# Rotation and copies of queries and keys one step sooner, 12 projection pieces ahead of the loop, mixing weights spread by matmuls

## The chip, the cores and the metric

The kernel runs on one core of one Trainium2 chip. The metric is device time in microseconds (us) of one execution. Beside three runs of the kernel before there is one more execution, taken with the hardware profiler; all durations below come from that one.

## What is computed

A decoder block over 2048 tokens of width 1024, all in float32: RMSNorm, one input projection, four heads of a gated linear recurrence (HGRN2), eight heads of causal dilated window attention, an output projection, the residual and a last RMSNorm. The change touches the attention part only:

```python
q = rope(at_q.reshape(B, S, AT_HEADS, AT_HEAD_DIM), positions)
k = rope(at_k.reshape(B, S, AT_HEADS, AT_HEAD_DIM), positions)
for window, dilation in ((128, 1), (512, 4), (2048, 16)):
    o_i, lse_i = dilated_window_attention(q, k, v, window, dilation)
mix_w = softmax(stack(lses), axis=0)
o_at = sum(mix_w * stack(outs)) * silu(at_z)
```

The kernel computes the windows of 512 and 2048 together as one "far" part, beside a "near" part for the window of 128, and mixes the two.

## The kernel before

**Stages.** A prologue normalises and transposes x and splits it into high and low halves (`u_hi`, `u_lo`). A second stage does the recurrence, beside its projections. A dense stage projects the values of the attention. Then comes the attention loop, and last the output projection. Every projection is three matmuls (high by high, high by low, low by high) for each of 8 slices of the contraction.

**The attention loop** goes over 64 steps `T`. Four steps `i` = 0 to 3 make a block `n` (16 blocks of 512 queries of two heads); four blocks `g` = 0 to 3 make a unit `v` (two heads). The far part of a query tile has `g`+1 key tiles, so steps grow longer with `g`.

Every engine runs its own loop over `T`, in the order in which it is written out, with semaphores between them:

- **TensorE (PE)**, in step `T`: `scores` (near at L758, far at L765) of tile `T`; transposes of the probabilities of tile `T`-1 (`turn_near_far0` at L781 and L789, `turn_far1` at L797); `weigh` of tile `T`-1 (L811, L819). Six "filler" pieces of projections stand between them, each three matmuls of 512 columns (L710 to L712): for block `n`+1 the pieces `A` and `B` (the two halves of queries and keys before rotation), for block `n` the pieces `Z` (the gate). `AHEAD` pieces run ahead of the loop, which sets where in a block each piece stands. They take turns between two PSUM banks: `B` of block `n` waits until the gate of block `n`-2 has been read (`z_done`), `Z` of block `n` until the first half of the rotation of block `n`+1 has been (`a_read`). In step `i` = 1 PE also spreads the mixing weights of the block before (`spread_weights`, L832).
- **VectorE (DVE)**: `lows` (masking, with row minima, L1488), `take_far0` (a PSUM copy), the rotation (`rope_a` in step 0, `rope_b` in step 1, both at L1251), `queries_keys_lo` (low halves, step 2), the mixing weights (`differences`, `mix_weights`, step 0), `weigh_outputs` (step 1), and the product that finishes the gate (L1566, step 3).
- **ScalarE (ACT)**: exponentials (L999), copies from PSUM (`take_near`, `take_far1`, `take_output`), `queries_keys_hi` (step 2), the tanh of the gate (L1055, step 3), high halves of the next unit's weights (`split_unit_hi`, L898), and it issues the copies of keys into `ks` (`gather_keys`, L316; step 2, in the last block of a unit step 3).
- **GpSimd (POOL)**: `combine` (step 1) and low halves of the next unit's weights (`split_unit_lo`, L1111).
- **SyncE (SP)** issues the other DMAs in one in-order queue. It waits for the end of PE's step (`pv_mm`) before it loads values (L461, L453) for the next. At the end of step 2 come the store of the output of block `n`-1 (`store_output`, L436), then the copies of the next block's queries into `qd` (L467), first half 0, then, past the scores of step 3, half 1; then the rotation table (L443). Far statistics go through DRAM at the end of step 3 and back in step 0 (L534, L507).

The tile `gate` is a single buffer: the tanh of block `n` waits until the store of block `n`-1 has landed (`comb_stored`), since `combine` leaves its result there. `r1`, `t1`, `t2`, `t3` share their room with `turned`, from which the copies read.

## Time and profile before

| what | value |
| --- | --- |
| runs of the kernel (3) | 1493.76, 1493.96, 1496.74 us; median 1493.96 us |
| profiled execution, its own time | 1488.3 us |
| its span, first to last instruction | 1486.5 us |
| busy share of the span | PE 91%, PE weight load 79%, DVE 52%, ACT 31%, POOL 21% |
| mean granted TensorE clock | 0.962 of full |
| attention loop, 659 to 1270 us | 611 us, granted clock 0.94 |

The profiled execution is 5.7 us faster than the median of the runs, and the 1.8 us between its time and its span lie outside of the instructions. "Busy" of PE counts a matmul from start to modelled end, so matmuls overlap in it. A row of the timeline gives the start, the time until the last of its instructions ends, and in brackets how long the engine was idle before, with what ended that.

### The profile page before, as it was taken

Reading aid. Unit: us, or ns where it says so; the run is one execution under the profiler, and the core shown is the slowest. Engines: PE = TensorE matmul, PEld = TensorE weight load, DVE = VectorE, ACT = ScalarE, POOL = GpSimd, SP = SyncE. Lnnn points to the kernel's source line nnn. Section 1 sums busy time; section 2 is a strip of 40 time slices with the busy share of each in tenths; the row PEclk is TensorE's granted clock in tenths of the full one; section 3 lists DMA queues with packets and bytes.
Section 4 is the critical chain, followed back from the end, with each engine's and each line's share of the span. In section 5 each row is a group of like instructions: output and inputs, shape, how many; then the busy total and the mean of one; then the engine's idle time right before and its main releaser. Section 6 shows DMA issues by size and latency. Waiting matters only on the chain.

```text
span 1486.5 us, 24236 instructions
## 1 busy us (share of the span) xinstructions
PE 1346.7 (91%) x8616; PEld 1174.3 (79%) x8616; DVE 774.7 (52%) x1933; ACT 466.4 (31%) x1328; POOL 314.8 (21%) x377
## 2 busy tenths in 40 slices
PE   5999989989999998899988888889988897599997
PEld 5989979989898998797767777677776776488886
DVE  6846847774783775215554455545555554332332
ACT  6622221122122121124444344434433444411221
POOL 5733333243243121100110002100111001110010
PEclk9999999999999999999999999999999999699999
DMA  6420230122022013413343334433323336434341
GB/s 199 144 73 22 72 103 19 43 76 78 31 76 79 22 49 102 121 38 77 106 116 92 83 101 115 99 77 89 90 70 85 83 90 196 144 112 143 128 138 61
DMA packets 115568, 135.39 MB, mean 91 GB/s; under 512 B 19584, under 2 KB 85376, under 8 KB 115456
## 3 DMA queue, kind: packets, MB, share of 16 engines
q1 hardware_dynamic: 109504, 121.81, 28.3%
q10 hardware_dynamic: 5952, 12.06, 2.8%
q8 instruction: 74, 1.21, 0.4%
q14 instruction: 38, 0.31, 0.1%
HBM read 79.18 MB, written 29.49 MB: 73 GB/s over the span
## 4 chain that ended last, share of the span: by engine, by line
PE 40%; DMA 8%; SPq 5%; DVE 3%; issue 1%; ACT 1%; ACTq 1%; POOL 0%; POOLq 0%; DVEq 0%
PE bank L577 5%; DMA qd<-turned 5%; PE bank L579 5%; PE bank L578 5%; PE bank L710 4%; PE bank L712 4%; PE bank L711 4%; SPq L467 3%; PE bank L765 3%; PE bank L819 3%; PE bank L758 2%; DVE o_nf L1251 2%; PE bank L811 2%; DMA ks<-turned 1%; PE bank L781 1%
## 5 line engine op out<-in xcount | busy, mean ns | idle before, releaser
L577 PE MATMUL bank<-w_hi,u_hi 128*128 128x256 f32 x768 | 222.4, 290 | 8.9 <-POOL w_lo L1104 4.8
L578 PE MATMUL bank<-w_lo,u_hi 128*128 128x256 f32 x768 | 219.0, 285 | 0.0
L579 PE MATMUL bank<-w_hi,u_lo 128*128 128x256 f32 x768 | 218.9, 285 | 0.0
L1488 DVE CUSTOM_DVE_ANT_0 p_near<-bank,near_m 128x256 f32<-128x256 f32 (+1 forms) x128 | 48.2, 414 | 259.9 <-PE bank L781 157.2
L577 PEld LDWEIGHTS bank<-w_hi,u_hi 128*128 128x128 f32 x768 | 149.0, 194 | 11.3 <-POOL w_lo L1104 5.3
L1251 DVE TENSOR_TENSOR room<-room 128x256 f32<-128x256 f32 (+6 forms) x386 | 136.0, 400 | 41.9 <-POOL room L1168 38.2
L578 PEld LDWEIGHTS bank<-w_lo,u_hi 128*128 128x128 f32 x768 | 149.1, 194 | 0.2
L579 PEld LDWEIGHTS bank<-w_hi,u_lo 128*128 128x128 f32 x768 | 148.9, 194 | 0.0
L710 PE MATMUL bank<-u_hi,w_hi 128*128 128x512 f32 x256 | 116.3, 454 | 4.0 <-issue 4.0
L1194 POOL TENSOR_TENSOR o_nf<-o_nf 128x512 f32<-128x512 f32 x16 | 25.5, 1591 | 420.5 <-DVE o_nf L1251 420.5
L1009 ACT COPY pT<-bank 128x512 f32<-128x512 f32 x60 | 35.2, 587 | 249.3 <-PE bank L781 226.3
L577 PE MATMUL bank<-wo_hi,mT_hi 128*128 128x512 f32 x256 | 101.9, 398 | 7.4 <-DVE mT_lo L1251 7.4
L577 PE MATMUL bank<-u_hi,w_hi 128*128 128x512 f32 x256 | 101.2, 395 | 7.9 <-issue 4.8
L712 PE MATMUL bank<-u_hi,w_lo 128*128 128x512 f32 x256 | 107.9, 421 | 0.0
L711 PE MATMUL bank<-u_lo,w_hi 128*128 128x512 f32 x256 | 107.4, 419 | 0.0
L758 PE MATMUL bank<-ks,qd 128*128 128x256 f32 (+1 forms) x256 | 53.9, 327 | 52.8 <-DMA qd<-turned 41.8
L579 PE MATMUL bank<-wo_hi,mT_lo 128*128 128x512 f32 x256 | 100.4, 392 | 0.0
L578 PE MATMUL bank<-wo_lo,mT_hi 128*128 128x512 f32 x256 | 100.3, 392 | 0.0
L579 PE MATMUL bank<-u_hi,w_lo 128*128 128x512 f32 x256 | 99.9, 390 | 0.0
L578 PE MATMUL bank<-u_lo,w_hi 128*128 128x512 f32 x256 | 99.7, 389 | 0.0
L765 PE MATMUL bank<-ks,qd 128*128 128x128 f32 (+3 forms) x256 | 92.5, 367 | 0.0
L758 PEld LDWEIGHTS bank<-ks,qd 128*128 128x128 f32 x256 | 37.7, 200 | 67.2 <-DMA ks<-turned 28.1
(164 smaller groups left out, 2958.8 us busy)
## 6 DMA issues: line engine op xcount, KB each, us to landing
qd<-turned SPq DMA_DIRECT2D x64, 256.0 KB, 5.8
stage<-in_w_groups SPq DMA_DIRECT2D x44, 256.0 KB, 3.9
room<-in_x SPq DMA_DIRECT2D x16, 512.0 KB, 4.4
values_gates<-vg_tile SPq DMA_DIRECT2D x64, 128.0 KB, 1.7
room<-values_gates SPq DMA_DIRECT2D x16, 512.0 KB, 4.5
tab<-in_rope SPq DMA_DIRECT2D x16, 512.0 KB, 6.1
xr<-in_x SPq DMA_DIRECT2D x16, 512.0 KB, 5.0
out<-hh SPq DMA_DIRECT2D x16, 512.0 KB, 3.0
```

Source lines behind the costliest of these rows:

```text
L467: sp.dma_start(qd[(2 * n + h) % Q_SLOTS][64 * z:64 * z + 64, :, :].bitcast(F32).rearrange("p a b -> p (a b)"), src[:, None, :].to_broadcas ...
L577: nc.tensor.matmul(dst, lhs_hi(k), rhs_hi(k), start=(k == 0), stop=False)
L578: nc.tensor.matmul(dst, lhs_hi(k), rhs_lo(k), start=False, stop=False)
L579: last = nc.tensor.matmul(dst, lhs_lo(k), rhs_hi(k), start=False, stop=(k == KT_N - 1))
L710: yield nc.tensor.matmul(bk[:, :], wh[:, k, :], u_hi[:, k, sl], start=(k == 0), stop=False)
L711: yield nc.tensor.matmul(bk[:, :], wh[:, k, :], u_lo[:, k, sl], start=False, stop=False)
L712: last = nc.tensor.matmul(bk[:, :], wl[:, k, :], u_hi[:, k, sl], start=False, stop=(k == KT_N - 1))
L758: last = nc.tensor.matmul(dst, q[h][:, z, j * P:(j + 1) * P], key_tiles(h, T), start=(z == 0), stop=(z == 1))
L765: last = nc.tensor.matmul(bank[2 + h][:, 0:P * (g + 1)], q[h][:, z, j::CH], keys, start=(z == 0), stop=(z == 1))
L819: last = nc.tensor.matmul(bank[6][hs, P:2 * P], far_v[:, far_slot(T, kk) % FAR_SLOTS, hs], pT[1 + h][:, kk, :], start=(kk == 0), stop=(kk ...
L1251: return nc.vector.tensor_tensor(dst, a_, b_, op)
L1488: nc.vector.tensor_tensor_reduce(out=dst, in0=src, in1=msk, scale=1.0, scalar=3e38, op0=ALU.add, op1=ALU.min, accum_out=stt[:, j, h:h + 1] ...
```

## The change

- `queries_keys_hi`, `queries_keys_lo`, the key copies of blocks other than a unit's last and the first half of the query copies move from step 2 to step 1; `rope_b` moves from step 1 to step 0, behind `mix_weights`.
- `mix_weights` leaves 128x8 weights in `ea` and `eb`, and no longer spreads them over 128x512. `spread_weights` does that by 16 matmuls, with a weight column repeated 64 times as the stationary operand and the identity as the moving one, in place of 8 transposes.
- The tanh of the gate moves from the middle of step 3 to the end of step 2 on ACT, and the product on DVE to the start of step 3. The store of the output stays at the end of step 2 on SP.
- `AHEAD` goes from 6 to 12 pieces. The rotation table's load and the next unit's weights (loads and splits) move with them.

```diff
@@ -284,7 +284,7 @@
         out_stored = [out_stored0, out_stored1]
 
         fill = filler_parts()
-        AHEAD = 6
+        AHEAD = 12
 
         def fillers(tile, first, many):
 
@@ -494,21 +494,17 @@
                 if i == 3 and n + 1 < AT_BLOCKS:
                     after(s_ready, 3 * T + 3)
                     gather_queries(n + 1, 1)
-                    if n + 2 < AT_BLOCKS:
-                        after(b_read, n + 2)
-                        load_table(n + 2)
-                if i == 3 and g == 1 and v + 1 < AT_UNITS:
-                    load_unit_piece(unit_pieces(v + 1)[0])
-                    load_unit_piece(unit_pieces(v + 1)[1])
                 if i == 0 and n >= 1:
                     after(stat_stored, 16 * n)
                     if n >= 3:
                         after(wts_ready, n - 2)
                     sp.dma_start(st_farn[(n - 1) % 2][:, :, :],
                                  stat_dram[n - 1].rearrange("(c t w) -> t c w", c=CH, w=4)).then_inc(stat_landed, 16)
-                if i == 0 and g == 3 and v + 1 < AT_UNITS:
-                    load_unit_piece(unit_pieces(v + 1)[4])
-                    load_unit_piece(unit_pieces(v + 1)[5])
+                if i == 1 and n + 1 < AT_BLOCKS:
+                    after(qk_lo, n + 2)
+                    if n >= 1:
+                        after(s_ready, 12 * n)
+                    gather_queries(n + 1, 0)
                 if T >= 1:
                     after(pv_mm, T)
                     load_far(T)
@@ -517,18 +513,16 @@
                             after(vg_stored[z], (DENSE + 2) * 128)
                     if T + 1 < AT_TILES:
                         load_near(T + 1)
-                if i == 2:
-                    if n >= 1:
-                        after(comb_done, n)
-                        store_output(n - 1)
-                    if n + 1 < AT_BLOCKS:
-                        after(qk_lo, n + 2)
-                        if n >= 1:
-                            after(s_ready, 12 * n)
-                        gather_queries(n + 1, 0)
-                    if g == 2 and v + 1 < AT_UNITS:
-                        load_unit_piece(unit_pieces(v + 1)[2])
-                        load_unit_piece(unit_pieces(v + 1)[3])
+                if i == 1 and n + 2 < AT_BLOCKS:
+                    after(b_read, n + 2)
+                    load_table(n + 2)
+                if i == 2 and n >= 1:
+                    after(comb_done, n)
+                    store_output(n - 1)
+                if v + 1 < AT_UNITS and (g, i) in ((1, 2), (2, 1), (2, 3)):
+                    z = ((1, 2), (2, 1), (2, 3)).index((g, i))
+                    load_unit_piece(unit_pieces(v + 1)[2 * z])
+                    load_unit_piece(unit_pieces(v + 1)[2 * z + 1])
                 if i == 3:
                     after(e_done, 4 * T + 4)
                     sp.dma_start(stat_dram[n].rearrange("(i w) -> i w", i=P),
@@ -823,13 +817,15 @@
             def spread_weights(n):
 
                 pe.wait_ge(wts_ready, n + 1)
-                for f, w in enumerate((r1, t3)):
+                for f, w in enumerate((ea, eb)):
                     if f == 0:
                         pe.wait_ge(pt_near_far1, 8 * (n + 1))
                     else:
                         pe.wait_ge(pt_far0, 4 * (n + 1))
                     for j in range(CH):
-                        last = nc.tensor.transpose(bank[4 + f][:, j * P:(j + 1) * P], w[:, j * P:(j + 1) * P], ident[:, :])
+                        for h in range(2):
+                            last = nc.tensor.matmul(bank[4 + f][HD * h:HD * h + HD, j * P:(j + 1) * P],
+                                                    w[:, j, h:h + 1].to_broadcast([P, HD]), ident[:, :], start=True, stop=True)
                     last.then_inc(wt_mm, 1)
 
             for T in range(AT_TILES):
@@ -1038,7 +1034,7 @@
                 v, g = divmod(n, BLOCKS)
                 if T >= 1:
                     take_near(T - 1)
-                if i == 2 and n + 1 < AT_BLOCKS:
+                if i == 1 and n + 1 < AT_BLOCKS:
                     queries_keys_hi(n + 1)
                 if T < AT_TILES:
                     exps(T, 0)
@@ -1048,22 +1044,22 @@
                     gather_keys(nc.scalar, n + 1)
                 if T >= 1:
                     take_far1(T - 1)
-                if i == 3:
-                    act.wait_ge(z_ready, n + 1)
-                    if n >= 1:
-                        act.wait_ge(comb_stored, 16 * n)
-                    nc.scalar.activation(gate[:, :], bank[filler_bank("Z", n)][:, :], ACT.Tanh, scale=0.5).then_inc(th_done, 1)
                 if i == 0 and 1 <= n < AT_BLOCKS:
                     exp_differences(n - 1)
                 if T < AT_TILES:
                     exps(T, 1)
                 if T >= 1:
                     take_output(T - 1)
-                if i == 2 and g != 3 and n + 1 < AT_BLOCKS:
+                if i == 1 and g != 3 and n + 1 < AT_BLOCKS:
                     act.wait_ge(qk_lo, n + 2)
                     gather_keys(nc.scalar, n + 1)
-                if v + 1 < AT_UNITS and (g, i) in ((2, 1), (2, 3), (3, 3)):
-                    z = ((2, 1), (2, 3), (3, 3)).index((g, i))
+                if i == 2:
+                    act.wait_ge(z_ready, n + 1)
+                    if n >= 1:
+                        act.wait_ge(comb_stored, 16 * n)
+                    nc.scalar.activation(gate[:, :], bank[filler_bank("Z", n)][:, :], ACT.Tanh, scale=0.5).then_inc(th_done, 1)
+                if v + 1 < AT_UNITS and (g, i) in ((2, 0), (2, 2), (3, 2)):
+                    z = ((2, 0), (2, 2), (3, 2)).index((g, i))
                     if z < 2:
                         act.wait_ge((a_ready, b_ready)[z], 4 * v + 4)
                     else:
@@ -1209,8 +1205,8 @@
                 v, g = divmod(n, BLOCKS)
                 if i == 1 and n >= 1:
                     combine(n - 1)
-                if v + 1 < AT_UNITS and (g, i) in ((2, 1), (2, 3), (3, 3)):
-                    z = ((2, 1), (2, 3), (3, 3)).index((g, i))
+                if v + 1 < AT_UNITS and (g, i) in ((2, 0), (2, 2), (3, 2)):
+                    z = ((2, 0), (2, 2), (3, 2)).index((g, i))
                     split_unit_lo(unit_pieces(v + 1)[2 * z])
                     split_unit_lo(unit_pieces(v + 1)[2 * z + 1])
                 for j in {AT_TILES - 2: (0,), AT_TILES - 1: (2,), AT_TILES: (4, 6)}.get(T, ()):
@@ -1515,12 +1511,9 @@
                 settle()
                 tick(nc.vector.reciprocal(den[:, :, :], den[:, :, :]))
                 settle()
-                def spread(w):
-                    return w[:, :, :].rearrange("p c h -> p (c h)")[:, :, None].to_broadcast([P, 2 * CH, HD])
-
-                for w, dst in ((ea, r1), (eb, t3)):
-                    last = nc.vector.scalar_tensor_tensor(out=dst[:, :].rearrange("p (n d) -> p n d", d=HD), in0=spread(w), scalar=0.5,
-                                                          in1=spread(den), op0=ALU.mult, op1=ALU.mult)
+                for w in (ea, eb):
+                    last = nc.vector.scalar_tensor_tensor(out=w[:, :, :], in0=w[:, :, :], scalar=0.5, in1=den[:, :, :],
+                                                          op0=ALU.mult, op1=ALU.mult)
                 last.then_inc(wts_ready, 1)
 
             def weigh_outputs(n):
@@ -1549,10 +1542,14 @@
                     restart()
                 if i == 1 and n >= 1:
                     weigh_outputs(n - 1)
+                if i == 3:
+                    dve.wait_ge(th_done, n + 1)
+                    nc.vector.scalar_tensor_tensor(out=gate[:, :], in0=gate[:, :], scalar=1.0, in1=bank[filler_bank("Z", n)][:, :],
+                                                   op0=ALU.add, op1=ALU.mult).then_inc(z_done, 1)
                 if i == 0 and n >= 2:
                     dve.wait_ge(stat_stored, 16 * (n - 1))
                 lows(T, 0)
-                if i == 2 and n + 1 < AT_BLOCKS:
+                if i == 1 and n + 1 < AT_BLOCKS:
                     queries_keys_lo(n + 1)
                 if T >= 1:
                     take_far0(T - 1)
@@ -1561,13 +1558,9 @@
                 if i == 0 and n >= 1:
                     differences(n - 1)
                 lows(T, 1)
-                if i == 3:
-                    dve.wait_ge(th_done, n + 1)
-                    nc.vector.scalar_tensor_tensor(out=gate[:, :], in0=gate[:, :], scalar=1.0, in1=bank[filler_bank("Z", n)][:, :],
-                                                   op0=ALU.add, op1=ALU.mult).then_inc(z_done, 1)
                 if i == 0 and n >= 1:
                     mix_weights(n - 1)
-                if i == 1 and n + 1 < AT_BLOCKS:
+                if i == 0 and n + 1 < AT_BLOCKS:
                     rope_b(n + 1)
                 if T == AT_TILES - 1:
                     out_weights_lo(1)
```

Where the instructions now stand, at three places of block 1 (`n` = 1, `g` = 1; numbers behind a name are buffers).

**DVE, from the end of step 0 into step 1.** `den` ends the mixing weights, `t3`, `r1`, `t1` are `rope_b`, `o_nf` is `weigh_outputs`. Before:

```order
L1516 RECIPROCAL den_98<-den_98 128x8 [waits dve_step]
L1522 SCALAR_TENSOR_TENSOR r1_78<-ea_96,den_98 128x512 [waits dve_step]
L1522 SCALAR_TENSOR_TENSOR t3_80<-eb_97,den_98 128x512
L1251 TENSOR_TENSOR o_nf_71<-o_nf_71,bank4 128x512 [waits wt_mm,o_read]
L1251 TENSOR_TENSOR o_nf_71<-o_nf_71,bank5 128x128x4 [waits wt_mm]
```

Now:

```order
L1512 RECIPROCAL den_98<-den_98 128x8 [waits dve_step]
L1515 SCALAR_TENSOR_TENSOR ea_96<-ea_96,den_98 128x8 [waits dve_step]
L1515 SCALAR_TENSOR_TENSOR eb_97<-eb_97,den_98 128x8
L1247 TENSOR_TENSOR t3_80<-bank0,tab_83 128x512 [waits a_read,b_ready]
L1247 TENSOR_TENSOR r1_78<-t1_77,t3_80 64x512 [waits dve_step]
L1247 TENSOR_TENSOR r1_78<-t1_77,t3_80 64x512
L1247 TENSOR_TENSOR t1_77<-bank0,tab_83 128x512 [waits dve_step]
L1247 TENSOR_TENSOR t3_80<-t1_77,t2_79 64x512 [waits b_read]
L1247 TENSOR_TENSOR t3_80<-t1_77,t2_79 64x512
L1247 TENSOR_TENSOR o_nf_71<-o_nf_71,bank4 128x512 [waits wt_mm,o_read]
L1247 TENSOR_TENSOR o_nf_71<-o_nf_71,bank5 128x128x4 [waits wt_mm]
```

The six instructions of `rope_b` now stand ahead of `weigh_outputs`; before they stood six rows behind it.

**ACT, end of step 2 and step 3.** `gate` is the tanh, `pT0` the copy `take_near`, `o_nf` the copy `take_output`. Before:

```order
L1009 COPY pT0_66<-bank4 128x512 [waits pv_mm,pt_mm]
L999 ACTIVATE p_near_69,st_near1_90<-p_near_69,st_near1_90 128x256 [waits s_taken] x2
L1015 COPY pT2_68<-bank4 128x256 [waits pv_mm,pt_mm]
L1055 ACTIVATE gate_88<-bank7 128x512 [waits comb_stored,z_ready]
L999 ACTIVATE p_far_86,st_far1_92<-p_far_86,st_far1_92 128x256 [waits s_taken] x2
```

Now:

```order
L1020 COPY o_nf_71<-bank6 128x2x128 [waits comb_done,pv_mm]
L1060 ACTIVATE gate_88<-bank7 128x512 [waits comb_stored,z_ready]
L1005 COPY pT0_66<-bank4 128x512 [waits pv_mm,pt_mm]
L995 ACTIVATE p_near_69,st_near1_90<-p_near_69,st_near1_90 128x256 [waits s_taken] x2
L1011 COPY pT2_68<-bank4 128x256 [waits pv_mm,pt_mm]
```

The tanh, with its wait on `comb_stored`, now stands ahead of every instruction of step 3.

**PE, step 3, behind `turn_near_far0`.** `p_near` and `p_far` are transposed, and `bank7` is that of the next filler piece. Now:

```order
L775 MATMUL bank4<-ident_57,p_near_69 128x128 [waits wt_read,pt_near_far1,e_done]
L775 MATMUL bank4<-ident_57,p_near_69 128x128 x3
L783 MATMUL bank5<-ident_57,p_far_86 128x128 [waits wt_read,pt_far0,e_done]
L783 MATMUL bank5<-ident_57,p_far_86 128x128
L704 MATMUL bank7<-u_hi_49,w_hi1_52 128x512 [waits z_done,b_read,lo_done]
```

This first piece of `B`, with its wait on `z_done`, stood at the same place in step 0 of the next block before.

## Rows read from the trace of the kernel before

**Rows 1.** The page: the chain that ended last, shares of the span by engine

```profile
PE 40%; DMA 8%; SPq 5%; DVE 3%; issue 1%; ACT 1%; ACTq 1%; POOL 0%; POOLq 0%; DVEq 0%
```

**Rows 2.** Groups by form, PE, 655 to 1290 us: near scores; busy, mean ns | idle before

```profile
L758 PE MATMUL bank<-ks,qd 128*128 128x256 f32 x240 | 51.3, 330 | 44.4 <-DMA qd<-turned 41.8 <-DMA ks<-turned 2.6
...
L758 PE MATMUL bank<-ks,qd 128*128 128x128 f32 x16 | 2.6, 283 | 8.4 <-DMA ks<-turned 8.4
```

**Rows 3.** Stretches after such waits: us, busy of each engine, PEclk, DMA share, GB/s

```profile
687.54:691.00 3.46, 3.46 (x12) 3.05 (x13) 0.00 (x0) 0.00 (x0) 0.00 (x0) 0.53 0.15 31
...
879.40:886.00 6.60, 6.60 (x22) 5.79 (x23) 0.93 (x5) 1.05 (x3) 0.00 (x0) 0.55 0.39 119
...
1239.34:1244.00 4.66, 4.66 (x15) 3.75 (x16) 0.00 (x0) 0.00 (x0) 0.00 (x0) 0.63 0.10 11
```

**Rows 4.** Timeline, PE, block 1, steps 0 and 1

```profile
691.20 0.60 PE L781 MATMUL bank<-ident,p_near 128*128 128x128 f32 x4
...
694.72 0.67 PE L811 MATMUL bank<-pT,near_v 128*64 128x128 f32 x8
695.21 0.40 PE L819 MATMUL bank<-pT,far_v 128*64 128x128 f32 x4
...
698.11 0.60 PE L832 MATMUL bank<-ident,r 128*128 128x128 f32 x4
...
699.68 0.60 PE L781 MATMUL bank<-ident,p_near 128*128 128x128 f32 x4
```

**Rows 5.** Timeline, DVE, `rope_b` of block 0, the first and last of 4 rows

```profile
668.68 0.69 DVE L1251 TENSOR_TENSOR t<-bank,tab 128x512 f32<-128x512 f32 x1
...
671.97 1.80 DVE L1251 TENSOR_TENSOR t<-t,t 64x512 f32<-64x512 f32 x2
```

**Rows 6.** Timeline, DVE, block 1, steps 0 and 1

```profile
691.95 0.42 DVE L1488 CUSTOM_DVE_ANT_0 p_near<-bank,near_m 128x256 f32<-128x256 f32 x1 [8.19 <-PE bank L789]
...
694.04 0.16 DVE L1251 TENSOR_TENSOR top<-st_near,st_farn 128x8 f32<-128x8 f32 x1
...
695.79 0.69 DVE L1522 SCALAR_TENSOR_TENSOR r<-ea,den 128x512 f32<-128x512 f32 x1
...
698.81 1.65 DVE L1251 TENSOR_TENSOR o_nf<-o_nf,bank 128x512 f32<-128x512 f32 x2 [1.72 <-PE bank L832]
```

**Rows 7.** Timeline, SP: the statistics' store, and the load behind it, block 15

```profile
1237.58 0.47 SPq L534 DMA_DIRECT2D far_stats<-st_far  x1
1241.39 0.36 SPq L507 DMA_DIRECT2D st_farn<-far_stats  x1
```

**Rows 8.** DMA issues, 655 to 1270 us: KB each, median us to landing

```profile
st_farn<-far_stats SPq DMA_DIRECT2D x15, 8.0 KB, 1.9
```

**Rows 9.** Timeline, PE, step 3 of block 5

```profile
867.77 0.75 PE L758 MATMUL bank<-ks,qd 128*128 128x256 f32 x4
...
869.65 0.40 PE L710 MATMUL bank<-u_hi,w_hi 128*128 128x512 f32 x1
...
870.35 0.60 PE L781 MATMUL bank<-ident,p_near 128*128 128x128 f32 x4
...
870.92 0.47 PE L710 MATMUL bank<-u_hi,w_hi 128*128 128x512 f32 x1
```

**Rows 10.** Timeline, SP: the output's store, same step

```profile
868.84 0.57 SPq L436 DMA_DIRECT2D attended<-gate  x1
```

**Rows 11.** The tile `attended`: time to landing of its DMAs

```profile
DMA to landing us min/median/max: 3.2/4.0/8.7
```

**Rows 12.** Timeline, ACT and DVE, the gate of block 5

```profile
873.49 0.60 ACT L1055 ACTIVATE gate<-bank 128x512 f32<-128x512 f32 x1 [0.21 <-DMA attended<-gate]
874.12 0.69 DVE L1566 SCALAR_TENSOR_TENSOR gate<-gate,bank 128x512 f32<-128x512 f32 x1 [0.78 <-ACT gate L1055]
```

**Rows 13.** Timeline, the next unit's weights split, two pieces each, ACT and POOL

```profile
899.45 1.14 ACT L898 CAST w_hi<-stage 128x512 fp32r<-128x512 f32 x2
...
759.68 2.48 POOL L1111 TENSOR_TENSOR w_lo<-stage,w_hi 128x512 fp32r<-128x512 f32 x2 [15.65 <-ACT w_hi L898]
```

## The prediction

> **What bounds the kernel now.** I began with the chain that ended last: PE 40%, DMA 8%, SP's queue 5% [rows 1]. Read with the table above (PE busy for 91% of the span, PE clock 0.94 in the attention loop), it says that PE sets the time, and that in the loop it stands still for DMAs. Everything moved here is in that loop, so only waits of PE and its clock count. The groups by form tell which: the near scores stood idle 44.4 us for copies of queries and keys in 240 matmuls, and 8.4 us in the 16 that begin a unit [rows 2]. All of it falls on block starts: 12 ordinary ones, 3.7 us each, and 3 unit starts, 2.8 us each. The view by stretches then shows the second price: after such a wait the granted clock is at or near 0.5, the lower of its two levels (1.2 GHz), for some microseconds of full work. The loss is length times one minus the clock: 1.6 us in the first row, 3.0 in the second, 1.7 in the last [rows 3]. There are 14 such stretches (after block 2's wait the clock held); worked out alike they lose 30.9 us, 25.8 of it at ordinary starts.
>
> **What is removed.** The keys and the first half of the queries leave a step earlier. The second half must wait for the scores of step 3, but only two copies are then in flight, not eight beside a table, and step 3 gets longer (below); I let it land in time. Gone: 44.4 + 25.8 = **70.2 us**.
>
> **Steps 0 and 1: the rotation ahead of the weighing.** `rope_b` takes 5.10 us on DVE (668.68 to 673.77) [rows 5], and what is queued behind it is `weigh_outputs`, which empties the banks for PE's next transposes. Count from PE's L781 in step 0 of block 1. DVE starts 0.75 later and reaches `differences` at 2.84 [rows 4, 6]. These need the far statistics, which go through DRAM. Their store is issued 1.07 us behind the end of step 3 (the output's store, in the same place of a step, is [rows 9, 10]), the load follows 3.81 later [rows 7], and lands in 1.9 [rows 8]: 6.78, less the 2.58 that scores take up to L781 [rows 9], is 4.20. Before, the wait at the block start hid this. Then 1.75 up to the spreads [rows 6]; two 128x8 products in place of two 128x512, 0.25 by the small row beside them [rows 6]; 5.10; and half of the 1.65 of `weigh_outputs` [rows 6]: 12.15. Before, L781 of step 1 came 8.48 behind that of step 0 [rows 4]. So **3.65 us** later, in 4 blocks of `g` = 1.
> The same sum for the others: `g` = 2 has longer PE steps, but in three of four POOL splits weights beside the rotation (4.2 each, the fourth 3.0); `g` = 3 gives 2.7 three times, having also two weight loads ahead of the statistics on SP; in `g` = 0 DVE is just in time and the spreads count, 1.1 three times; block 15 rotates nothing. With 1.1 for the last spread in the tail: 14.6 + 12.6 + 3.0 + 8.1 + 3.3 + 1.1 = **43 us**. From below, with statistics that land before DVE asks, a `g` = 1 block costs 2.3, and all of it 25.
> The spreads: 16 matmuls with 64 stationary columns. The nearest row is L811, four of them, recorded as 8, in 0.49 [rows 4], or 0.122 each: 1.96, against 0.87 for the 8 transposes (698.11 to L781 at 699.68, less a piece of 0.70) [rows 4, 9]. From below it is 1.52 by the pace of transposes, six in the 0.57 from 870.35 on, 0.095 each [rows 9]. I take the nearest row, 1.1 more per block; where DVE is late PE has time for it, and it costs nothing further.
> In step 1 `queries_keys_lo` also stands ahead of the copy that `weigh` needs, with one filler piece fewer to cover it than in step 2: about 0.4, 14 times, **5.6 us**. Between nothing and one piece of 0.70 [rows 9].
>
> **Step 3: the gate ahead of its store.** This is the wait that I weigh most. ACT now does the tanh before all of step 3, and it needs `comb_stored`. SP still issues that store at the end of step 2: 1.07 us after PE began step 3 [rows 9, 10]. It lands in 3.2 us at best, 4.0 in the median [rows 11]; fewer copies are beside it now, so 3.4. Then tanh 0.60 and DVE's product 0.69 [rows 12], and 0.15 for semaphores: 5.9. With 12 pieces ahead, the first piece of `B` stands right here on PE and waits for that product, and PE arrives at 3.15 [rows 9]. Wait: 2.8 at `g` = 1, 2.95 at `g` = 0. Before, the tanh sat late in step 3 and had 0.21 to wait [rows 12]. In three blocks of `g` = 2 that piece needs the next unit's weights, whose split is queued behind the tanh: 1.07 + 3.4 + 0.60 + half of 1.14 + 2.48 [rows 13] + 0.2 = 8.3, against an arrival at 3.5: 4.8. Block 0 has no store to wait for, block 14 no `B`. 4 x 2.8 + 3 x 2.95 + 3 x 4.8 = **34.5 us**, between 3.2 and 4.0 of landing 32 to 41.
>
> **Clock.** Ten waits of near 3 us or more in step 3, and three in step 1 that stay long after the spreads have filled part of them. The stretches after 14 of 15 block starts, which waited 3.5 us on average (52.8 over 15) [rows 2], lost 1.6 to 3.1; I take the low end, 13 x 1.75 = **23 us**. Below: nothing; above: 3.0 each.
> **The rest.** Six pieces of 0.70 [rows 9] now run ahead of the loop, and at its end the steps without pieces wait for ACT and DVE anyhow: **4.1 us**, between 0 and 4.1. At unit starts keys can't leave sooner (they overwrite `ks`); fewer copies beside them, but ACT issues them behind the late tanh: **-2.4 us**, between -15 and +5. All of the DVE time saved by small products lies in a wait of DVE on PE (1.72) [rows 6] and is worth nothing by itself.
>
> **Sum.** 43 + 5.6 + 34.5 + 23 + 4.1 - 2.4 - 70.2 = +37.6. From the profiled execution's 1488.3 this is 1526; it ran 5.7 us under the median of the runs, and beside that median, 1494.0, the prediction is **1532 us**.
>
> **A rule weighed.** Of the price of a spread, the row says 0.122 us for a float32 matmul with 64 stationary columns, against 0.095 for a transpose [rows 4, 9]. The Trainium skill, "TensorE: Matmul & The Clock Gate", Terms, says that the transpose mode is four times faster for float32, which would make a plain matmul four times as dear; the sum by it is that of rival 5.
>
> **Rivals.**
> 1. *Both waits, but the clock holds.* Block 2's start kept it, and the new waits come piecewise, with matmuls between. Without the 23: +15, 1509. Against it: 14 of 15 starts lost it [rows 3]. 0.20.
> 2. *Faster: the gate comes in time.* If the product is done 3.15 us into step 3 and not at 5.9, its 34.5 and 18 of clock vanish: -15, 1479. It decides at 2.8 us sooner. For it: ACT hardly waited for this store before. Against: it stood later then, and even the fastest landing, 3.2, gives 5.7. 0.12.
> 3. *Deeper clock.* The low stretches last as in the second of rows 3, at 20 waits, 3.0 each: 60 for 23, +75: 1569. 0.13.
> 4. *The change doesn't do what it says:* the second half of the queries still lands last, half of today's 3.7 at 12 starts: +22, 1554. For it: it is issued no sooner than before. 0.05.
> 5. *Dear spreads.* Each as four transposes, 0.38 to 0.4: 16 take 6.4, 5.5 more a block. DVE's lateness covers 3.7 of it at `g` = 1, 4.2 or 3.0 at 2, 2.7 at 3, 1.1 at 0 and in block 15 and the tail: about 44 more, 1576. This is the page's rule carried out; the row at 0.122 speaks against it. 0.03.
>
> **The numbers.** The forecast has 0.47. 0.2% (3 us) is about what a measurement of this kernel can tell from no change. Slower: the forecast and rivals 1, 3, 4, 5 less 0.03 from the low edge of rival 1; same 0.03; faster 0.12, rival 2. The range goes from 1495, which leaves rival 2 out and takes in the low ends of landing and clock, to 1570, which takes in rival 3.
>
> **What would show it.** Right: PE's near scores wait under 10 us for copies; the filler of L704 to L706 in step 3 waits for DVE's product, 2 to 5 us, and L775 in step 1 for `o_nf`, 1 to 3 us; ACT's gate is released by the store `attended`, 3 us and more in each block; the spreads take about 2 us; stretches at half clock stand in steps 3 and 1. Wrong: no wait on the product at the first piece of `B`, statistics that land before DVE asks, or copies that are still last at block starts.

## The result, and the profile after

| | kernel before | changed kernel |
| --- | --- | --- |
| median of the runs | 1494.86 us (4: 1493.76 to 1496.74) | 1516.48 us (4: 1512.70 to 1523.19) |
| ratio, 95% interval | 1 | **1.0148**, 1.0110 to 1.0186 |
| profiled execution, its own time / span | 1488.3 / 1486.5 us | 1517.36 / 1515.5 us |
| mean granted TensorE clock | 0.962 | 0.972 |
| attention loop: first near scores to the first transposes of the output projection (L862 before, L858 now) | 658.7 to 1285.7 us: 627 us | 663.7 to 1313.9 us: 650 us |

The change makes the kernel slower by 1.5%, 21.6 us by the medians. The forecast said slower, 1532 us, in a range of 1495 to 1570. Profile against profile it is +29.0 us where I had +37.6.

The page of the changed kernel, chain by engine (against [rows 1]):

```profile
PE 35%; DMA 7%; DVE 7%; ACT 3%; issue 3%; ACTq 2%; SPq 2%; POOL 1%; DVEq 0%; POOLq 0%
```

DVE's share rose from 3 to 7%, that of DMAs hardly moved: the chain now runs through DVE's products. In the view of waits of PE (engine, line, what for, us in total, times, longest), 655 to 1320 us:

```profile
PE bank L704 <- DVE gate L1547: 24.4, 10, 3.1
PE bank L704 <- POOL w_lo L1107: 17.2, 3, 7.0
PE bank L813 <- issue: 12.9, 14, 1.2
PE bank L791 <- ACT pT L1005: 12.9, 14, 4.4
PE bank L704 <- DVE t L1247: 10.1, 14, 0.9
PE bank L775 <- DVE o_nf L1247: 4.3, 6, 1.2
```

and in the groups by form of the same stretch:

```profile
L752 PE MATMUL bank<-ks,qd 128*128 128x256 f32 x240 | 45.7, 314 | 0.0
L752 PE MATMUL bank<-ks,qd 128*128 128x128 f32 x16 | 2.5, 281 | 0.0
L1060 ACT ACTIVATE gate<-bank 128x512 f32<-128x512 f32 x16 | 9.6, 598 | 64.7 <-DMA attended<-gate 64.7
```

The near scores (L752, before L758) never wait for a copy: the 44.4 and 8.4 us of [rows 2] are gone. In their place stand the first filler piece of `B` in step 3 (L704), which waits for the gate's product and, three times, for the next unit's low halves; the first piece of `Z` in step 0 (L704 for `t`); and the far weighing of step 1 (L813). ACT's tanh (L1060) waits for the store of `attended` in 15 blocks, 4.3 us each. One block's step 3 shows how:

```profile
718.61 1.00 SPq L436 DMA_DIRECT2D attended<-gate  x1
...
722.54 0.60 ACT L1060 ACTIVATE gate<-bank 128x512 f32<-128x512 f32 x1 [4.55 <-DMA attended<-gate]
723.17 0.69 DVE L1547 SCALAR_TENSOR_TENSOR gate<-gate,bank 128x512 f32<-128x512 f32 x1 [7.49 <-ACT gate L1060]
...
724.00 0.47 PE L704 MATMUL bank<-u_hi,w_hi 128*128 128x512 f32 x1 [3.11 <-DVE gate L1547]
```

Read from the bottom: PE stands 3.11 us for a product that DVE did within 0.69 us of the tanh, which stood 4.55 us for a store issued at 718.61. In a block with a weight split, it is worse, since ACT's and POOL's splits follow the tanh:

```profile
924.03 0.47 SPq L436 DMA_DIRECT2D attended<-gate  x1
...
929.38 0.60 ACT L1060 ACTIVATE gate<-bank 128x512 f32<-128x512 f32 x1 [6.50 <-DMA attended<-gate]
929.87 1.13 ACT L894 CAST w_hi<-stage 128x512 fp32r<-128x512 f32 x2
...
930.56 2.50 POOL L1107 TENSOR_TENSOR w_lo<-stage,w_hi 128x512 fp32r<-128x512 f32 x2 [18.62 <-ACT w_hi L894]
933.11 0.79 PE L704 MATMUL bank<-u_hi,w_hi 128*128 128x512 f32 x1 [7.00 <-POOL w_lo L1107]
```

The clock by stretches (us, busy PE, PEld, DVE, ACT, POOL, PEclk, DMA share, GB/s), against [rows 3]: it still falls, but behind these waits.

```profile
767.00:771.00 4.00, 3.72 (x12) 2.96 (x12) 0.15 (x1) 0.26 (x1) 0.22 (x1) 0.57 0.00 0
...
1057.00:1061.00 4.00, 4.00 (x14) 3.08 (x12) 1.21 (x7) 2.25 (x9) 0.00 (x0) 0.57 0.25 68
```

Busy time times one minus the clock, in steps of 1 us, sums to 34.6 us in the loop before (16 stretches) and to 25.9 now (14: ten in step 3 with 17.2 us, four in the last steps with 8.7).

**Where the 29 us came from.** The time from the near scores of a step to those of the next, summed by step over the 62 intervals and set against the same sums before: step 1 +38.0 us, step 2 +2.1, step 3 +22.7, step 0 -40.8; together +22.0. The loop begins 5.0 later, and 2.0 come after it. (Before, the near scores are split by their own wait, so part of it counts to step 3 and part to step 0; the two are best read together, -18.1.)

### The profile page after: what moved, and what is told of

It is laid out like the page before. It is cut to its first block, busy times and chain, and to the rows that moved or that the text cites. A ratio compares the mean times of both kernels' runs of the same rounds, so it can differ in the third digit from the quotient of the medians.

```text
span 1515.5 us, 25004 instructions
## 1 busy us (share of the span) xinstructions
PE 1365.1 (90%) x9000; PEld 1181.7 (78%) x9000; DVE 768.7 (51%) x1933; ACT 465.1 (31%) x1328; POOL 321.3 (21%) x377
## 4 chain that ended last, share of the span: by engine, by line
PE 35%; DMA 7%; DVE 7%; ACT 3%; issue 3%; ACTq 2%; SPq 2%; POOL 1%; DVEq 0%; POOLq 0%
PE bank L571 5%; PE bank L573 5%; PE bank L572 5%; PE bank L704 4%; DMA attended<-gate 3%; PE bank L706 3%; PE bank L705 3%; PE bank L813 3%; DVE t L1247 2%; ACTq L316 2%; PE bank L805 2%; DMA far_stats<-st_far 1%; PE bank L827 1%; PE bank L752 1%; PE bank L791 1%
## 5 line engine op out<-in xcount | busy, mean ns | idle before, releaser
L704 PE MATMUL bank<-u_hi,w_hi 128*128 128x512 f32 x256 | 114.7, 448 | 45.5 <-DVE gate L1547 24.4
L704 PEld LDWEIGHTS bank<-u_hi,w_hi 128*128 128x128 f32 x256 | 52.7, 206 | 54.0 <-issue 31.0
L1247 DVE TENSOR_TENSOR hh<-bank,xr 128x512 f32<-128x512 f32 x32 | 20.6, 686 | 129.2 <-PE bank L573 129.2
L759 PE MATMUL bank<-ks,qd 128*128 128x128 f32 (+3 forms) x256 | 86.0, 344 | 0.0
```

Source lines behind the costliest of these rows:

```text
L704: yield nc.tensor.matmul(bk[:, :], wh[:, k, :], u_hi[:, k, sl], start=(k == 0), stop=False)
L759: last = nc.tensor.matmul(bank[2 + h][:, 0:P * (g + 1)], q[h][:, z, j::CH], keys, start=(z == 0), stop=(z == 1))
L1247: return nc.vector.tensor_tensor(dst, a_, b_, op)
```

## The experiments

Each kernel ran 5 to 12 times, between runs of the kernel before on the same chip, and so each time stands beside a ratio to it. The experiments took four chips, so where two kernels lie close together, their ratios say more than their times. The theory was that of the forecast: the waits in step 3 come from the place of the attended store, and the clock goes with them.

**1. The attended store a step sooner.** On SP:

```diff
                 if i == 1 and n + 2 < AT_BLOCKS:
                     after(b_read, n + 2)
                     load_table(n + 2)
-                if i == 2 and n >= 1:
+                if i == 1 and n >= 1:
                     after(comb_done, n)
                     store_output(n - 1)
```

> The changed kernel with the store of the attended rows issued at the end of SP's step 1 (behind the table's load) and no longer behind the far and near loads of step 2. Theory (the gate is late because its tanh waits for that store to land): ACT's 15 waits of the tanh on the attended store (64.7 us in the changed kernel) fall under 10 us, DVE's gate waits on ACT (116.8 us) by at least 40 us, PE's waits at the first filler matmul of the B piece in step 3 for the gate product (24.4 us in ten blocks) fall under 3 us; the 17.2 us for the splits of the next unit's weights stay; some 10 to 13 us of half clock go with the waits. 1516.5 - 24 - 12 = about 1480 us, so faster than the kernel before (1494.9). Rival (the tanh would be late anyway, behind what ACT does in step 2): PE's wait shrinks by less than half and the time is 1505 us or more. A kernel time above 1516 would say that the earlier store delays the loads behind it.

Measured: 1477.2 us, ratio 0.9907 (0.9877 to 0.9936), so faster than the kernel before. The waits of PE:

```profile
PE bank L704 <- POOL w_lo L1107: 8.3, 3, 2.9
PE bank L704 <- DVE gate L1547: 7.2, 7, 1.3
```

One queued store was worth 39 us by the medians, 36 by the two ratios. By span it is 43.5, of which 41.2 lie in step 3, and two numbers make these up: the waits of L704 for gate and low halves fell by 26.1 us, the clock's loss in step 3 from 17.2 to 1.7. The time came out as expected, the waits did not go as far: ACT's for the store stayed at 23.4 us (expected under 10), PE's for the gate at 7.2 (expected under 3). The low halves, which I had left out of this expectation, came sooner too, since they queue behind the same tanh. What is left of ACT's wait (10 blocks) goes with a longer landing, 5.4 us in the median against 3.5. The store now leaves beside the key copies; that these lengthen its landing is not shown by itself.

**2. The spread alone,** put into the kernel before: the change's hunks in `mix_weights` and `spread_weights`, nothing else.

```diff
-                for f, w in enumerate((r1, t3)):
+                for f, w in enumerate((ea, eb)):
...
-                        last = nc.tensor.transpose(bank[4 + f][:, j * P:(j + 1) * P], w[:, j * P:(j + 1) * P], ident[:, :])
+                        for h in range(2):
+                            last = nc.tensor.matmul(bank[4 + f][HD * h:HD * h + HD, j * P:(j + 1) * P],
+                                                    w[:, j, h:h + 1].to_broadcast([P, HD]), ident[:, :], start=True, stop=True)
```

> The kernel before with only the mixing weights changed: DVE makes 2 small products in ea and eb, PE spreads them by 16 matmuls of 64 stationary columns a block in place of 8 transposes; the order of all else is that of the kernel before. Theory: the 16 matmuls take 1.9 us a block against 0.87 of the transposes, so 15 times about 1.0 = +15 us on PE, and DVE's side is shorter by about the two big products (they fall from some 0.7 us each to 0.1), which takes nothing off the path: 1494.9 + 10 to 15 = 1505 to 1510 us. Rival (PE waits at the spread now for DVE's products, and their shortening gives the time back): no change, 1493 to 1497. Rival (float32 matmuls cost four times a transpose): spreads of 3.5 us or more a block and 1535 us or more.

Measured: 1504.35 us, ratio 1.0087 (1.0057 to 1.0118): +13 us, between 8.5 and 18, so the theory, 1 us under its range. The 16 matmuls:

```profile
736.00 1.09 PE L833 MATMUL bank<-ident,ea 128*64 128x128 f32 x16
736.92 1.04 PE L833 MATMUL bank<-ident,eb 128*64 128x128 f32 x16
```

The rows overlap and count each matmul twice (32 for 16). In the changed kernel a spread starts at 786.11 and the next piece at 788.01: 1.90 us for 16, where 8 transposes had taken 0.79 (774.93 to 775.72). So 1.1 us a block, the size I had taken; 15 of them are 16.6 us, within what was measured. Here no lateness of DVE covers them.

**3. The splits ahead of the tanh.** On ACT, the splits keep their place and the tanh goes behind them:

```diff
-                if i == 2:
-                    act.wait_ge(z_ready, n + 1)
-                    ...
-                    nc.scalar.activation(gate[:, :], ..., ACT.Tanh, scale=0.5).then_inc(th_done, 1)
                 if v + 1 < AT_UNITS and (g, i) in ((2, 0), (2, 2), (3, 2)):
...
                     split_unit_hi(unit_pieces(v + 1)[2 * z + 1])
+                if i == 2:
+                    act.wait_ge(z_ready, n + 1)
+                    ...
+                    nc.scalar.activation(gate[:, :], ..., ACT.Tanh, scale=0.5).then_inc(th_done, 1)
```

> The changed kernel with ACT's two splits of the next unit's weights ahead of the tanh in step 2 of the blocks g = 2 and g = 3. Theory: the three waits of PE for the low halves on POOL (17.2 us: 4.7, 7.0, 5.4) go, since the splits no longer stand behind the tanh that waits for the store to land; what is left there is the wait for the gate product, 1.5 to 3 us each: -17.2 + 3 times 2.5 = -10 us, 1507 us (1503 to 1511). Rival (the splits' stages themselves land late, or the tanh is now late behind the splits): PE waits as long in these three blocks for the gate, and the time is 1514 or more.

Measured: 1507.9 us, ratio 1.0111 (1.0074 to 1.0147), as expected.

```profile
PE bank L704 <- DVE gate L1547: 31.8, 13, 3.2
PE bank L791 <- ACT pT L1005: 14.9, 13, 4.9
```

The wait for low halves is gone, and that for the gate rose from 24.4 to 31.8 us, by 2.5 in each of the three blocks, as expected.

**4. Ten pieces ahead.** In the changed kernel:

```diff
-        AHEAD = 12
+        AHEAD = 10
```

> The changed kernel with 10 filler pieces ahead of the loop in place of 12, so that the first piece of B in step 3, which waits for the gate product, stands behind the transposes of the second far scores, and B of the next block is complete at the end of step 0. Theory: the waits of PE for the gate product (24.4 us) go down to under 8 us and those for the low halves (17.2) to under 10, with some 8 us of half clock; DVE waits for B in step 0 up to 2 us longer, and PE's scores of step 1 wait up to 1 us in 15 blocks. 1516.5 - 16 - 7 - 8 + 10 = 1496 us (1488 to 1508). Rival (the rotation in step 0 now ends late, and near scores and weighing of step 1 wait for it): gives back all, 1516 or more.

Measured: 1489.6 us, ratio 0.9975 (0.9952 to 0.9999).

```profile
PE bank L791 <- ACT pT L1005: 32.3, 27, 5.2
PE bank L775 <- DVE o_nf L1247: 14.0, 11, 1.8
```

Lower than I had it by 6 us, with a surprise inside. No wait for the gate is left on PE, and 2.5 us for the low halves, but ACT still stands 64.3 us for the store, and now its other work shows: L791, the transposes that need ACT's copy of the near ones, waits 32.3 us against 12.9. The tanh at the head of ACT's queue holds back whatever is behind it.

**5. The gate back in its old place, ten pieces ahead.** Against experiment 4, on ACT and DVE:

```diff
                 if T >= 1:
                     take_far1(T - 1)
+                if i == 3:
+                    ...
+                    nc.scalar.activation(gate[:, :], ..., ACT.Tanh, scale=0.5).then_inc(th_done, 1)
...
-                if i == 2:
-                    ...
-                    nc.scalar.activation(gate[:, :], ..., ACT.Tanh, scale=0.5).then_inc(th_done, 1)
...
                 lows(T, 1)
+                if i == 3:
+                    dve.wait_ge(th_done, n + 1)
+                    nc.vector.scalar_tensor_tensor(out=gate[:, :], ...)
```

> The changed kernel with 10 filler pieces ahead and with the tanh and the gate product where the kernel before had them (ACT ahead of the second far exponentials of step 3, DVE behind the second far scores' minima). Theory (the gate's place hangs on how many pieces are ahead: the first B piece of step 3 waits for the product, and a product at the end of DVE's step 3 is too late for it): PE waits 2 to 3 us for the gate product in each of 14 blocks and loses 1.5 us of clock with each: the 1489.6 of the kernel with 10 ahead + 35 to 60 = 1525 to 1550 us. Rival (with 10 ahead the old place is early enough): 1487 to 1500 us.

Measured: 1496.5 us, ratio 1.0009 (0.9993 to 1.0025): the rival's range, not mine.

```profile
PE bank L704 <- DVE gate L1559: 31.8, 14, 4.2
...
PE bank L791 <- ACT pT L1005: 8.1, 13, 2.8
```

The wait for the gate came as expected (14 times, 2.3 us). What I left out is that the tanh no longer waits for the store (0.8 us), so L791 gave back 24.2 us and most of the price was paid. With ten pieces the early gate is worth 0.3%, some 5 us by the two ratios (between 1 and 9 with their intervals): it takes 31.8 us of waits for the gate off PE, and behind the tanh that waits for its store 24.2 of them come back.

**6. DVE's copy ahead of the subtractions in step 1.**

```diff
-                if i == 1 and n + 1 < AT_BLOCKS:
-                    queries_keys_lo(n + 1)
                 if T >= 1:
                     take_far0(T - 1)
+                if i == 1 and n + 1 < AT_BLOCKS:
+                    queries_keys_lo(n + 1)
```

> The changed kernel with DVE's copy of the turned first far scores ahead of the two subtractions of the queries' and keys' low halves in step 1. Theory: PE's wait of 0.92 us before the far weighing in 14 steps (12.9 us, which the trace gives no releaser) is the copy standing behind these subtractions, of which the second takes 1.8 us beside POOL; it goes, and the copies of queries and keys start 0.4 us later, which nothing on PE feels: 1516.5 - 12.9 = 1504 us (1501 to 1508). Rival (it is PE's own sequencer, or the waits go into the gate's wait two steps later): the wait stays, or comes back at the gate product in step 3, and the time is 1513 or more.

Measured: 1509.3 us, ratio 1.0090 (1.0061 to 1.0118), just over the expected range. L813's 12.9 us without a releaser are gone, so they were this copy. But 7 us came, not 13. By steps against the changed kernel: step 1 -16.5, step 2 +11.1, step 3 -5.7. Step 2 now waits for ACT's copy (L791: 20.3 us against 12.9):

```profile
750.24 0.60 ACTq L316 DMA_DIRECT2D ks<-turned  x1
...
750.87 1.64 ACTq L316 DMA_DIRECT2D ks<-turned  x1
...
752.54 1.88 ACTq L316 DMA_DIRECT2D ks<-turned  x2
...
754.52 0.59 ACT L1005 COPY pT<-bank 128x512 f32<-128x512 f32 x1 [3.29 <-issue]
...
755.25 0.52 PE L791 MATMUL bank<-ident,p_far 128*128 128x128 f32 x3 [0.37 <-ACT pT L1005]
```

ACT issues the four key copies at the end of step 1, which takes it 4.2 us; a shorter step 1 uncovers that. Neither of my two theories had it.

**7. The rotation a step later again,** all else as changed: `rope_b` in step 1, the splitting and copies in step 2, SP's gathers and table where they were.

```diff
-                if i == 1 and n + 1 < AT_BLOCKS:
+                if i == 2 and n + 1 < AT_BLOCKS:
                     queries_keys_hi(n + 1)
...
-                if i == 1 and g != 3 and n + 1 < AT_BLOCKS:
+                if i == 2 and g != 3 and n + 1 < AT_BLOCKS:
                     act.wait_ge(qk_lo, n + 2)
                     gather_keys(nc.scalar, n + 1)
...
-                if i == 1 and n + 1 < AT_BLOCKS:
+                if i == 2 and n + 1 < AT_BLOCKS:
                     queries_keys_lo(n + 1)
...
-                if i == 0 and n + 1 < AT_BLOCKS:
+                if i == 1 and n + 1 < AT_BLOCKS:
                     rope_b(n + 1)
```

> The changed kernel with the rotation of the queries and keys back in step 1, their splitting and copies back in step 2 and SP's gathers and table load where they were; the early tanh, 12 pieces ahead and the spreading by matmuls stay. Theory (the earlier rotation by itself is a gain, which the other parts of the change outweigh): the waits of the near scores for copies come back at 45 to 55 us with 15 to 20 us of half clock, 10 to 13 us before the far weighing go: 1516.5 + 50 + 8 - 12 = about 1560 us (1545 to 1575). Rival (the earlier rotation is worth nothing, since the gate's wait takes the place of that for the copies): 1500 to 1525 us.

Measured: 1538.2 us, ratio 1.0303 (1.0271 to 1.0335), 22 us above the changed kernel and so between theory and rival.

```profile
PE bank L704 <- DVE gate L1547: 32.1, 11, 4.0
PE bank L704 <- DVE t L1247: 19.9, 26, 1.5
PE bank L704 <- POOL w_lo L1107: 19.6, 3, 6.6
...
PE bank L752 <- DMA ks<-turned: 6.9, 3, 2.8
```

The near scores wait 8.5 us in all (6.9 and 1.6 for queries), not 50. The gate's wait in the step before gives the copies the time that they lack. So the two waits overlap: with the gate late, the sooner rotation is worth 22 us, and not the 52.8 us of waits with their clock. The two profiles differ by 16.6 us, and PE's waits by 15.5 of it: gate and low halves 51.7 us for 41.6 (the tanh waits 72.0 us for its store, not 64.7), the bank that the rotation still reads 19.9 for 10.1, the copies 8.5, less the 12.9 at L813.

**8. Four repairs at once:** the store ahead of the queries' gather in SP's step 1, the splits ahead of the tanh, the copy of experiment 6, and 11 pieces ahead. The splits and the copy are the diffs of experiments 3 and 6; the others:

```diff
-        AHEAD = 12
+        AHEAD = 11
...
+                if i == 1 and n >= 1:
+                    after(comb_done, n)
+                    store_output(n - 1)
                 if i == 1 and n + 1 < AT_BLOCKS:
                     after(qk_lo, n + 2)
...
-                if i == 2 and n >= 1:
-                    after(comb_done, n)
-                    store_output(n - 1)
```

> The changed kernel with four repairs at once: the attended store ahead of the queries' gather in step 1 of SP; ACT's splits of the next unit's weights ahead of the tanh; DVE's copy of the first far scores ahead of the subtractions in step 1; 11 filler pieces ahead. Theory (the waits are of separate causes and PE is the bound): the waits for the gate product (24.4 us), the low halves (17.2), the keys' rotation before the first gate piece (10.1) and before the far weighing (12.9) go but for some 8 us, and 17 us of half clock with them: 1516.5 - 56 - 15 = 1445 us (1436 to 1458). Rival (another engine is next: ACT's copy before the second far transposes, or a transfer): 1465 us or more, with PE waits for ACT of over 25 us.

Measured: 1458.95 us, ratio 0.9758 (0.9733 to 0.9784), 2.4% faster than before and 58 us below the changed kernel. The tanh never waits (0.0 us on the store), and neither does PE for the gate.

```profile
PE bank L791 <- ACT pT L1005: 14.3, 16, 1.9
PE bank L775 <- DVE o_nf L1247: 10.2, 11, 1.4
PE bank L813 <- DMA far_v<-values: 10.1, 6, 4.4
...
PE bank L704 <- POOL w_lo L1107: 5.7, 3, 2.0
```

It is 14 us over the expectation and 1 us outside its range: step 2 again takes 12.7 us more than in the changed kernel. I put that down to ACT's issues, as in experiment 6; experiment 11 tests it.

**9 and 10. Two variations of it:** the third filler piece of step 1 ahead of the near transposes, in the diff, and `AHEAD = 10`.

```diff
                     spread_weights(T // CH - 1)
-                    for f in fillers(T, 2, 1):
+                    for f in fillers(T, 2, 2):
                         filler(*f)
...
-                for f in fillers(T, 3, 1) if mixes else fillers(T, 2, 2):
+                for f in fillers(T, 4, 1) if mixes else fillers(T, 2, 2):
...
-                for f in fillers(T, 4, 2):
+                for f in fillers(T, 5, 1) if mixes else fillers(T, 4, 2):
```

> The kernel with the four repairs, and in step 1 the third filler piece ahead of the near transposes in place of behind them (two pieces between the spread and the near transposes, one between near and second far transposes, one before the weighing). Theory: the waits of the near transposes for DVE's product with the spread weights (10.2 us in 11 steps, up to 1.4) go, the second far transposes in step 1 wait up to 0.5 us longer for ACT's copy: 1459 - 10 + 4 = 1453 us (1449 to 1458). Rival (the wait only moves to the later transposes): 1458 to 1464.

> The kernel with the four repairs, but 10 pieces ahead in place of 11. Theory: the waits for the low halves (5.7 us in three blocks) go, but B of the next block is complete only at the end of PE's step 0, DVE's rotation comes later and holds up the products in step 1, as in the changed kernel with 10 ahead (there 14 us before the near and 32 before the second far transposes): 1459 - 6 - 4 + 10 to 25 = 1459 to 1474 us. Rival (those waits came of the late gate alone): 1450 to 1457 us.

Measured: 1458.7 us, ratio 0.9754 (0.9726 to 0.9783), and 1461.7, ratio 0.9776 (0.9747 to 0.9804). The first is the rival's case: the wait for DVE's product fell from 10.2 to 4.1 us, those for ACT's copies (L791 and L813) rose from 18.4 to 24.4. With ten pieces L775 waits 14.9 us and the low halves 1.2, and the time lies in the theory's range. Neither time can be told from that of experiment 8.

**11. The key copies off ACT's queue.** In the kernel of experiment 8, for blocks other than a unit's last, from the end of ACT's step 1 to SP's step 1 behind the far and near loads:

```diff
-                if i == 1 and g != 3 and n + 1 < AT_BLOCKS:
-                    act.wait_ge(qk_lo, n + 2)
-                    gather_keys(nc.scalar, n + 1)
...
+                if i == 1 and g != 3 and n + 1 < AT_BLOCKS:
+                    gather_keys(sp, n + 1)
```

> The kernel with the four repairs, and the copies of the keys of a unit's first three following blocks issued by SP behind the far and near loads of step 1 in place of ACT's queue. Theory: four issues hold ACT for 4.3 us at the end of step 1 and make its copy of the turned near scores late in step 2; PE's waits there before the second far transposes (about 1.1 us in most blocks, 14.3 us in all) fall under 7, and the far load of step 1, issued beside ACT's own, is no longer slowed: 1459 - 8 - 2 = 1449 us (1445 to 1454). Rival (SP's queue is then the late one: the table and the loads of step 2 behind four more issues, PE waits for values): 1457 us or more.

Measured: **1451.9 us**, ratio 0.9725 (0.9693 to 0.9757), the lowest of all; expected 1449. By the ratios that is 0.3% under experiment 8, and the two intervals overlap, so the gain in time is not clear of noise.

```profile
PE bank L754 <- DMA qd<-turned: 4.6, 3, 2.2
PE bank L793 <- ACT pT L1007: 3.8, 5, 1.9
```

The wait for ACT's copy (L793 in its numbering) fell from 14.3 to 3.8 us; 4.6 us for query copies are new. Against the changed kernel step 2 is 1.7 us shorter, not 12.7 longer. So ACT's issues were what held step 2.

## Why the prediction was right, and where it was off

- **What is removed, 70.2.** The waits went as said, and 8.4 us more: at unit starts I had let the keys stay late (-2.4), and they are in time. They are so in experiment 1 as well, without long waits in step 3; which of the lighter queues did it, no run separates.
- **Steps 0 and 1, 43 + 5.6.** 38.0 us measured in step 1, and much of it is made of other parts. The far statistics are hardly late: their store is issued at 729.35 and the load at 731.92, 2.6 us where I took 3.81 from block 15 [rows 7]. Over the 15 blocks that gap was 2.7 to 6.7 us in the kernel before and is 2.3 to 3.6 now. Why it shrank stays open: in experiment 7, with the copies back in their place, it is 2.1 to 3.6 as well. DVE waits for the statistics 5 us in the whole loop, in the second of these rows; that they land before DVE asks was one of my signs of being wrong, and in most blocks they do.

```profile
DVE p_near L1484 <- DMA far_stats<-st_far: 40.7, 7, 6.1
DVE top L1247 <- DMA st_farn<-far_stats: 5.0, 7, 1.4
```

The first row is not a wait for them, whatever its name: `lows` in step 0 asks only for the store of the block before last, and in all seven blocks DVE starts 0.77 or 0.78 us behind L775, as it started 0.75 behind L781 before [rows 4, 6]. So DVE's lateness, which was most of the 43, shows as 4.3 us before L775. What filled its place: the spreads at 1.1 in 15 blocks (16.6), which I had hidden behind that lateness, and the copy behind `queries_keys_lo`, priced 0.4 and measured 0.92 (12.9), because its second subtraction takes 1.78 us beside POOL where the first takes 0.69. Some 4 us of the 38.0 stand in no row of waits. That 38.0 lies near 48.6 is therefore mostly luck. In step 0 comes a wait that I did not see at all, 10.1 us: with 12 pieces ahead, the first `Z` piece stands there and needs the bank that `rope_a` still reads.

```profile
779.93 0.47 PE L704 MATMUL bank<-u_hi,z_hi 128*128 128x512 f32 x1 [0.72 <-DVE t L1247]
...
786.11 1.09 PE L827 MATMUL bank<-ident,ea 128*64 128x128 f32 x16
787.03 1.04 PE L827 MATMUL bank<-ident,eb 128*64 128x128 f32 x16
...
789.44 0.63 PE L775 MATMUL bank<-ident,p_near 128*128 128x128 f32 x4 [0.47 <-DVE o_nf L1247]
```

- **Step 3, 34.5.** 41.6 us measured, with the chain as forecast: store, landing (3.5 us in the median, taken 3.4), tanh, product, PE. At `g` = 1 PE waits 3.1, 2.6, 2.7 and 2.6 us against 2.8, at `g` = 0 2.2 to 2.5 against 2.95. The three splits took 5.7 each, not 4.8: the longest wait of the tanh, 6.50, is in one of them. The waits at `g` = 3 (1.6 to 2.5 us) I had left out.
- **Clock, 23.** 17.2 us in ten step 3s, behind waits of 2.0 to 7.0 us; three others, of 1.6, 2.5 and 3.1 us, cost no clock. It did not fall in step 1, where the waits are short. Experiment 1 shows that it hangs on these waits: with those for the gate at 1.3 us and less and three for low halves of up to 2.9, one stretch of the ten is left. Rival 1, that the clock holds, is out; so is rival 3: its 3.0 us came once (3.01, near the loop's end), not 20 times.
- **Rival 2,** the gate in time, did not happen, but its mechanism did decide: experiment 1 brings the store forward and makes the kernel faster. That its 1477.2 lies beside the rival's 1479 is luck: the rival took 53 us off 1532, the run 39 off 1516, with 15.5 us of these waits left.
- **Rival 4** is out: no near scores wait. **Rival 5** is out. The trace disagrees with the Trainium skill, "TensorE: Matmul & The Clock Gate", Terms: a matmul of the spread costs 0.119 us (1.90 over 16) against 0.099 for a transpose (0.79 over 8), a factor of 1.2 where the page has four for the transpose mode in float32, without saying against what.

By steps the account closes: step 1 38.0 for 48.6; steps 3 and 0 together -18.1 for 34.5 + 23 - 2.4 - 70.2 = -15.1; step 2 +2.1 for nothing; ahead of the loop and behind it 7.0 for 4.1. That is 8.6 us less, as measured. The term that failed is DVE's lateness in step 1: the statistics arrive sooner than the gap of block 15 made them, and 4.3 us of it are left. In steps 3 and 0 errors cancel: the waits of step 3 (7.1 us over) and the one before `Z` (10.1) stand against the clock (5.8 under) and the unit starts (6.0 us of keys that I had let stay late, and the 5.1 of clock that went with them, 30.9 less 25.8).

## What to carry to other kernels

Before a step is moved ahead of another, list what it waits for and where *that* is issued: here a tanh moved one step forward and the store that it needs stayed, at a price of some 36 to 39 us. A wait at the head of an in-order queue is paid by everyone who needs what stands behind it, so look at the waits of the moved instruction's engine and not at PE's alone. And waits in one step overlap: taking one away shows the next, and only runs that remove them together show what is to be had; here the whole change, slower by 1.5% as first written, became 2.8% faster with its repairs. How much of that is the sooner rotation stays open, since no run has the repairs without it.

## What the runs showed of the hardware

The issue of a DMA took its queue longer when copies were being issued around it. SP issues a far and a near load in 1.0 us in step 2 (717.60 and 718.01 in the changed kernel); in step 1, behind the query copies and beside ACT's keys, the same two take it 3.1:

```profile
709.59 0.61 ACTq L316 DMA_DIRECT2D ks<-turned  x1
709.74 1.04 SPq L461 DMA_DIRECT2D far_v<-values  x1
710.23 3.64 ACTq L316 DMA_DIRECT2D ks<-turned  x3
710.82 2.03 SPq L453 DMA_DIRECT2D near_v<-values  x1
```

With all of them on SP (experiment 11):

```profile
709.69 1.01 SPq L461 DMA_DIRECT2D far_v<-values  x1
710.74 1.32 SPq L453 DMA_DIRECT2D near_v<-values  x1
712.11 2.51 SPq L316 DMA_DIRECT2D ks<-turned  x4
```

Far, near and keys are out 4.9 us after the first of them began (709.69 to 714.62), against 4.3 us on two queues (709.59 to 713.87), and the keys' issue takes 2.5 us in all and not 4.25. The Trainium skill, "DMA: Bandwidth & Descriptors", Issuing engines are not separate DMA queues, says that starting DMAs on several engines saves only the sequencer's time; here that gave SP 1.8 us back (it is busy with issues 3.1 us and not 4.9) and had all six transfers out 0.6 us sooner, bought with 4.3 us of ACT.
